# Two-block transformer forward pass on one core: a weight tile loaded later, the first query product in halves, a closing step moved

## The reference, cut to what matters

```python
query = (ht @ w_query).reshape(t, 8, 2, 128)              # 1024 -> 2048
sub_scores = einsum('thpd,hpkd->thpk', query, sub_keys)
half_vals, half_idx = top_k(sub_scores, 16)
cand = half_vals[:, :, 0, :, None] + half_vals[:, :, 1, None, :]
top_vals, top_pos = top_k(cand.reshape(t, 8, 256), 16)
experts = i1 * 128 + i2                                   # from half_idx and top_pos
gates = softmax(top_vals)
u = expert_down[experts]                                  # 1024 numbers per expert
act = gelu(einsum('td,thkd->thk', x, u), approximate=False) * gates
y = einsum('thk,thkd->td', act, expert_up[experts])
x = x + gt2 * y ; x = rms_norm(x, g_final)
```

## Time and profile before

| | |
|---|---|
| median of 3 runs | 1640.22 us (1640.17 to 1643.65) |
| the profiled execution | 1638.71 us, span 1636.9 us |
| TensorE busy | 1363.7 us (83%) |
| VectorE busy | 1105.7 us (68%) |
| ScalarE busy | 530.1 us (32%) |
| GpSimd busy | 380.5 us (23%) |
| DMA | 433.17 MB, 264 GB/s over the span |
| of it the gathers | 268.45 MB, 39.8% of 16 engines' span |
| the chain that ended last | TensorE 47%, DMA 25%, VectorE 20%, ScalarE 5% |

### The profile page before, as it was taken

One profiled execution on the slowest core, in us unless ns is written; L12 is line 12 of the kernel. 1 busy time (PEld: TensorE's weight loads), 2 busy tenths in 40 slices (PEclk: granted clock), 3 DMA queues, 4 the chain that ended last, 5 costly groups with the idle time before them and its releaser, 6 DMA issues.

```text
span 1636.9 us, 17137 instructions
## 1 busy us (share of the span) xinstructions
PE 1363.7 (83%) x6234; PEld 954.1 (58%) x6234; DVE 1105.7 (68%) x2021; ACT 530.1 (32%) x1024; POOL 380.5 (23%) x329
## 2 busy tenths in 40 slices
PE   6999778777767776777777778978999999899997
PEld 6887658523222222322222237867999877689996
DVE  6575574588888688888455555566765578867654
ACT  1443342222221123222111133542544254534430
POOL 1000001244444344444344411100111033001110
PEclk9999888999999999999999999999999999999999
DMA  9554525799999999999999963324465443355550
GB/s 366 203 206 154 206 78 206 275 422 405 422 421 416 417 421 406 367 422 421 421 421 421 420 265 138 120 77 168 169 206 182 173 164 109 123 180 206 182 179 26
DMA packets 116628, 433.17 MB, mean 265 GB/s; under 512 B 6832, under 2 KB 7088, under 8 KB 83520
## 3 DMA queue, kind: packets, MB, share of 16 engines
q0 software_dynamic: 36864, 268.45, 39.8%
q1 hardware_dynamic: 79392, 162.51, 28.0%
q10 hardware_dynamic: 288, 1.11, 0.2%
HBM read 431.00 MB, written 1.05 MB: 264 GB/s over the span
## 4 chain that ended last, share of the span: by engine, by line
PE 47%; DMA 25%; DVE 20%; ACT 5%; issue 2%; SPq 0%; POOL 0%; DVEq 0%; ACTq 0%; POOLq 0%
PE PS L45 45%; DMA EB<-in_experts,EI 24%; DVE EB L78 5%; DVE WL L75 4%; ACT BIG L24 2%; PE PS L84 1%; DVE LNV L63 1%; DVE Y L75 1%; DVE GV L75 1%; DMA W<-in_w_ada 1%; DVE X L63 1%; DVE XL L75 1%; ACT WH L24 1%; ACT EB L24 1%; DVE ST L69 1%
## 5 line engine op out<-in xcount | busy, mean ns | idle before, releaser
L45 PE MATMUL PS<-EB,BIG 128*128 128x512 f32 x1024 | 489.1, 622 | 168.1 <-ACT BIG L24 168.0
L45 PEld LDWEIGHTS PS<-EB,BIG 128*128 128x128 f32 x1024 | 188.8, 195 | 464.9 <-ACT BIG L24 284.5
L39 POOL DMA_INDIRECT EB<-in_experts,EI x256 | 289.6, 1131 | 602.0 <-PE PS L45 399.6
L78 DVE CUSTOM_DVE_ANT_0 EB<-EB,Y 128x1024 f32<-128x1024 f32 x256 | 313.5, 1224 | 137.4 <-DMA EB<-in_experts,EI 136.5
L75 DVE TENSOR_TENSOR WL<-W,WH 128x1024 fp32r<-128x1024 f32 x240 | 308.6, 1335 | 130.5 <-ACT WH L24 130.1
L24 ACT ACTIVATE WH<-W 128x1024 fp32r<-128x1024 f32 x240 | 237.2, 1048 | 79.5 <-PE PS L45 72.8
L45 PE MATMUL PS<-XH,WH 128*128 128x256 f32 x832 | 241.7, 291 | 11.1 <-DVE WL L75 10.5
L45 PE MATMUL PS<-XH,WL 128*128 128x256 f32 x832 | 235.5, 283 | 0.0
L45 PE MATMUL PS<-XL,WH 128*128 128x256 f32 x832 | 235.4, 283 | 0.0
L24 ACT ACTIVATE BIG<-BIG 128x2 f32<-128x2 f32 (+1 forms) x136 | 31.1, 228 | 444.9 <-DVE BIG L78 444.5
L45 PEld LDWEIGHTS PS<-XH,WH 128*128 128x128 f32 x832 | 159.8, 192 | 14.8 <-DVE WL L75 12.1
(11 more groups left out here) (170 smaller groups left out, 1405.4 us busy)
## 6 DMA issues: line engine op xcount, KB each, us to landing
W<-in_ffn_w SPq DMA_DIRECT2D x32, 2048.0 KB, 8.9
W<-in_w_ada SPq DMA_DIRECT2D x12, 2048.0 KB, 12.6
W<-in_w_in SPq DMA_DIRECT2D x6, 2048.0 KB, 12.8
W<-in_hy_w_in SPq DMA_DIRECT2D x6, 2048.0 KB, 13.7
W<-in_gla_w_in SPq DMA_DIRECT2D x6, 2048.0 KB, 7.9
W<-in_w_query SPq DMA_DIRECT2D x4, 2048.0 KB, 10.6
W<-in_w_out SPq DMA_DIRECT2D x2, 2048.0 KB, 8.0
EB<-in_experts,EI POOLq DMA_INDIRECT x256, 10.8
```

The source lines that it names most:

```text
L39: return lambda e: e.indirect_dma_start(*a, **k)
L45: return lambda e: e.matmul(*a, **k)
L78: return lambda e: e.tensor_tensor_reduce(*a, **k)
```

## The change

1. The tile held back is `hyt[2]` instead of whatever goes into W3. Since the list is in order, `hyt[3]` stays behind it. `hyt[2]` may be loaded when the last gather has landed.
2. The first query product of the first tile is made in two halves of 256 columns, each with its own copies, transposes and scores. Only the first half is needed for the first choice; the second half is issued behind that choice. One split piece of `wq[1]` stands ahead of the query's first copy instead of behind its second.
3. The closing of the first tile (`fin`) starts its steps only when all experts are chosen.

```diff
-        held = [3]
+        held = [hyt[2].index]
...
-                if t.before_w is not None and t.before_w.done is None or t.s == held[0] and t.index >= first_block_tiles:
+                if t.before_w is not None and t.before_w.done is None or t.index == held[0]:
                     return
...
-        def score(t, j, tq):
+        def score(t, j, tq, i0=0, i1=4):
             b = bank()
-            for i in range(4):
+            for i in range(i0, i1):
...
-        def first_query(t, xt):
-
-            b = bank()
-            tk = dense(PS[b][:, :], wq[0], tm_pairs(wq[0], t), *xt, *bank_free[b])
...
+        def first_query(t, xt, parts):
+
+            n = 4 // parts
+            ts = slice(t * 128, (t + 1) * 128)
+            for p in range(parts):
+                c, i0 = slice(p * n * 128, (p + 1) * n * 128), p * n
+                b = bank()
+                tk = dense(PS[b][:, c], wq[0], lambda k: parts3((XH[:, k, ts], XL[:, k, ts]), (wq[0].hi[:, k, c], wq[0].lo[:, k, c])),
+                           *xt, *bank_free[b])
...
+                ta = act(lambda e: e.activation(STG[:, c], PS[b][:, c], ACT.Copy), tk, t_wout, *(stg_free if t else ()), ordered=False)
+                bank_free[b] = (ta,)
+                yield
+                b = bank()
+                for i in range(i0, i0 + n):
+                    tk = tr(PS[b][:, i * 128:(i + 1) * 128], STG[:, i * 128:(i + 1) * 128], ta, *bank_free[b])
...
+                yield
+                yield score(t, 0, tq, i0, i0 + n)
...
-        query = first_query(0, (norm_x1.xt[0],))
+        query = first_query(0, (norm_x1.xt[0],), 2)
+        later_split(wq[1])
+        tick(1)
         next(query)
-        later_split(wq[1])
         later_split(wq[2])
         next(query)
-        tick(1)
         norm_x1.last()
         t_xt = norm_x1.tokens
         next(query)
         for step in choose(0, 0, 1):
             step()
+        for _ in query:
+            pass
         drain()
...
-        query = first_query(1, t_xt)
+        query = first_query(1, t_xt, 1)
...
-                next(fin, None)
+                if chosen:
+                    next(fin, None)
...
         held[0] = None
...
-        w_free[hyt[3].index] = e_free[1]
+        w_free[hyt[2].index], w_free[hyt[3].index] = (landed[total - 1],), e_free[1]
         load_on()
```

More of the change, by code:

```diff
@@ L1145, in score @@
             ts = act(lambda e: e.activation(
-                BIG[:, 4096 + t * 2048 + j * 512:4096 + t * 2048 + (j + 1) * 512], PS[b][:, :], ACT.Copy), tk, ordered=False)
+                BIG[:, 4096 + t * 2048 + j * 512 + i0 * 128:4096 + t * 2048 + j * 512 + i1 * 128],
+                PS[b][:, i0 * 128:i1 * 128], ACT.Copy), tk, ordered=False)
             bank_free[b] = (ts,)
@@ L1151, in build @@
         stg_free = []
-        def first_query(t, xt):
-            b = bank()
-            tk = dense(PS[b][:, :], wq[0], tm_pairs(wq[0], t), *xt, *bank_free[b])
[L1157 to L1170, removed]
+        def first_query(t, xt, parts):
[6 more added lines that the diff above has]
+                           *xt, *bank_free[b])
+                if t:
+                    wdone(wq[0], tk)
+                ta = act(lambda e: e.activation(STG[:, c], PS[b][:, c], ACT.Copy), tk, t_wout, *(stg_free if t else ()), ordered=False)
[4 more added lines that the diff above has]
+                    tk = tr(PS[b][:, i * 128:(i + 1) * 128], STG[:, i * 128:(i + 1) * 128], ta, *bank_free[b])
+                stg_free[:] = [tk]
+                tq = act(lambda e: e.activation(QT[0][:, i0:i0 + n, ts], PS[b][:, c].rearrange("p (c t) -> p c t", c=n), ACT.Copy),
+                         tk, t_wout, ordered=False)
+                bank_free[b] = (tq,)
+                yield
+                yield score(t, 0, tq, i0, i0 + n)
         def top16(src, vals, idx, *tokens):
```

## The result

The changed kernel takes 1626.55 us in the median of 4 runs (1623.73 to 1628.1), the kernel before 1640.2 us beside it (1637.11 to 1643.65, 4 runs). The ratio is 0.9918, with a 95% interval of 0.9902 to 0.9933: 13.4 us shorter, 11.0 to 16.1. Forecast were 1624.3 us and 15.9 us shorter.

A forecast was written before the change was run, and what follows sets the result against it. The prediction took the 16 DMA engines, full at 421 to 422 GB/s in the expert stage's gathers, as the bound. Terms 5.0 + 0.6 + 6.4 + 3.9 = 15.9 us off 1640.2 gave 1624.3 us, range 1618 to 1632.

The forecast's parts named there:

- The prediction's own sign: From the first full DMA stretch to the last landing: wrong if not some 12 us shorter, or if the tail grows.
- The tile and the last gather: End of the expert stage: held tile's 2.097 MB leave it, minus 5.0 us; last gather no longer shares engines, minus 0.6.
- the smaller term: Last gather: without the W3 load beside it, the last two dot products' 3.10 us spacing becomes 2.49, minus 0.6 us.
- The cover of 27.0 us: After the last gather's landing: 27.0 us until ScalarE's first split of the held tile, hiding that tile's load.
- Rivals 3 and 4: Held tile: 3, it only used gaps between gathers, 1629.3 us, chance 0.05; 4, it lands late, 1635.8 us, chance 0.03.
- The halves: Before the stage: first head's choice needs only half the query columns, so choosing starts at about 240.8 us, minus 3.9 us.
- Rival 1: Query product: TensorE's clock eats the halves' gain, 1628.2 us, or 1631.7 at half clock throughout; chance 0.12.
- The closing: DMA dip at 650 to 685 us, worth 6.9 us: holding the closing until all is chosen removes it, net minus 6.4 us.
- a new dip: Closing's new place, about 776 us: 0.5 us allowed for lost DMA time, the rest covered by VectorE's free time and queued gathers.
- Rival 2: Closing: the dip moves with it, because its own serial waits starve the gathers, not the choosing's company; 1630.7 us, chance 0.10.

The follow-up runs named there:

- the spread closing: Each closing step one slot behind the other-engine step it needs: on the changed kernel (new place) 1624.36 us; on the kernel before (old place) 1636.72 us.
- the closing alone: The kernel before with only the closing of the first tile's sum put later, until all experts are chosen: 1637.89 us, ratio 0.9992.
- the edit that moved nothing: The changed kernel with SyncE's load of constants meant to issue 20 slots later, but the load did not move: 1626.89 us, ratio 0.9928.
- two tiles held: The changed kernel with the second weight tile, `hyt[1]`, also held behind the last gather: 1622.51 us, ratio 0.9894.

## Why the prediction was right, and where not

**The total** was right within 2.3 us and the sign with it. By its terms it was less right: two held and one fell short. The prediction's own sign for that was a stage some 12 us shorter; it is 8.3 us shorter (656.65 to 648.34). That the total came out so near was in part luck: the closing fell 3.8 to 5.1 us short, and the tile's time (6.7 us against 5.6) and the halves' (4.1 against 3.9) lay a little above their terms.

**The tile and the last gather**, 5.0 + 0.6 = 5.6 us forecast: 5.15 us of stage alone, 6.7 us (4.4 to 8.9) of time. The last two dot products stand 2.42 to 2.47 us apart in the traces with the tile held and 3.10 to 3.14 in the others, as the smaller term had it. The cover of 27.0 us was there. Rivals 3 and 4 fall for this tile. Where the prediction weighed the Trainium skill's 358 GB/s a core (DMA: Bandwidth & Descriptors, Specifications) against the trace, an estimate by that rate would be 6.5 us; by the stage the 421 GB/s of the trace gave the nearer number, while the interval of the time holds both. The Trainium skill's figure is a stack's rate halved between two cores, and here only one was at work, so the two did not contradict each other as the prediction had it.

**The halves**, 3.9 us forecast: 4.1 us (2.6 to 5.6) alone. Choosing starts 4.05 us earlier beyond the head's own variation, and the second wait for the split ends at 251.38 instead of the 252.9 forecast. Rival 1 falls: the clock was lower behind the choice in one of the two traces shown, and choosing and the gather of slot 6 came earlier in both. The rule that the prediction set beside it, bursts that start slow again behind waits (the Trainium skill, TensorE: Matmul & The Clock Gate, HAM oscillation — how this bites in real kernels), did not take the gain here. The 0.50 in the spread closing behind a wait of 4.32 us, with a burst of 3.70 us ahead of it, agrees with it; the 0.50 behind 3.22 us, with 9.68 us of matmuls ahead, is no case of it.

**The closing**, 6.4 us forecast: 1.3 us alone, 2.6 us by its undoing. This is the step that failed, at two sentences. "Choosing alone causes no dip, the two together do" took the company of VectorE for the cause; the spread closing kept that company, with VectorE busier, and 650 to 685 us ran at 419 GB/s. And "I take 0.5 us for a new dip" counted VectorE's free time at the new place and the gathers in flight, but not what the other engines' queues hold: there VectorE has time (9.70 of 15 us busy from 785 to 800), and gathers wait 5.26 and 5.44 us for TensorE, which waits for ScalarE, where steps of the closing stand in line ahead of the products. These rows show how the gathers come late; that the line is the whole cause at the new place is not shown, since the spread closing, in which ScalarE first waits for a transpose at 792.66 us, kept the fall. The new fall measured 3.2 us in the changed kernel and 3.4 us in the closing alone. Rival 2, that the dip moves along because of the closing's own serial waits, was right that about half of the dip moves along and that the company of the choosing isn't its cause; it had a chance of 0.10 and deserved more, since the row of GpSimd's wait for TensorE spoke for it and the count of VectorE's time did not speak against it.

**The sum.** The terms measured alone are 6.7 + 4.1 + 1.3 = 12.1 us, against 13.4 (11.0 to 16.1) together: they add up within the intervals. The profiled execution's 15.0 us, so near the 15.9, were partly the head's 1.3 us that no edit made.

**What stays open:** what makes the fall at the new place. With the closing spread, the low clock behind TensorE's waits is seen there and the load of constants stands beside it; no run has that closing there without either. At the old place it stays open whether spreading helps by readiness or by thinning the closing out.

## What to carry to other kernels

In this ring of gathers, which runs at the DMA engines' limit, the busy share of an engine did not tell what work beside the gathers costs: VectorE was busier in the stretch without the fall. A step that waits for another engine held the ring's own step behind it, and moving the whole block elsewhere moved about half of the loss with it. Look first at the releaser chain of one late gather (GpSimd for TensorE, TensorE for ScalarE, ScalarE for VectorE). What won each time here is fewer bytes in the stage: each load that can wait for the last gather, as far as the tail covers it, gave back 4 to 5 us per 2.1 MB.

## What the runs showed of the hardware

- Two profiles of the changed kernel (the second with the edit that moved nothing) start the first choice at 239.36 and 241.74 us, 2.4 us apart, while their stages are 648.34 and 648.83 us: the head varied between executions, the DMA-bound stage hardly.
- TensorE was granted 0.50 behind a wait of 4.32 us in the middle of the stage, and 0.50 behind one of 3.22 us, while a pause of 2.89 us kept 1.00 in the stretch at 288 us. The wait's length alone does not tell: the same 3.0 us in the same program had a slow burst behind it in one execution (776.99 us above) and a fast one in the other (780.35); with the closing back at its old place, too, 640 to 645 us ran at 0.50 while the DMA engines moved 264 GB/s:

```profile
640.00:645.00 5.00, 5.00 (x7) 1.93 (x6) 4.66 (x11) 4.24 (x10) 0.94 (x1) 0.50 0.66 264
```

- Of three weight tiles issued together behind the last gather (948.79 us, two tiles held), the first had landed within 9.8 us, the time that its first split left.
